# Scaling the residual on GpSimd in two passes, and two more early rounds of the search

## The reference

```python
x = x + _mixers(_rmsnorm(x, g_attn), w_in, g_out_a, g_out_b, sink_a, rpb_b, w_out)
h = _rmsnorm(x, g_ffn).reshape(B * S, D)      # (tokens, 1024)
return x + _expert_choice_ffn(h, w_router, w_gate, w_up, w_down).reshape(B, S, D)

def _expert_choice_ffn(h, w_router, w_gate, w_up, w_down):
    N, D = h.shape
    cap = CAP_FACTOR * N // N_EXPERTS         # 128 for the sample, 64 for the prompt
    aff = jax.nn.softmax(jnp.einsum('nd,de->ne', h, w_router).astype(jnp.float32), axis=-1)
    gate, idx = lax.top_k(aff.T, cap)
    xe = h[idx]
    ...
```

## Time and profile before

| | us |
|---|---|
| three runs | 2481.93, 2485.30, 2485.79 |
| median | 2485.3 |
| the profiled execution | 2484.71 |
| its span in the profile | 2482.9 |
| mixing, from its first own work to its last closing round | about 502 to 682 |
| the rest of the choice, up to the gather | about 682 to 696 |

### The profile page before, as it was taken

One profiled execution on the slowest core, in us unless ns is written; L12 is line 12 of the kernel. 1 busy time (PEld: TensorE's weight loads), 2 busy tenths in 40 slices (PEclk: granted clock), 3 DMA queues, 4 the chain that ended last, 5 costly groups with the idle time before them and its releaser, 6 DMA issues.

```text
span 2482.9 us, 43086 instructions
## 1 busy us (share of the span) xinstructions
PE 2434.5 (98%) x16395; PEld 2178.7 (88%) x16395; DVE 1673.5 (67%) x2432; ACT 1456.5 (59%) x2050; POOL 163.7 (7%) x172
## 2 busy tenths in 40 slices
PE   9999999999889999999999999999999999999997
PEld 7888877777579989899998989999998989999896
DVE  6355278854776767676666767666676767666677
ACT  4332189977555656556565656555565655656574
POOL 0000000000010101101010100101010110101010
PEclk9999999999989999999999999999999999999998
DMA  7353255354376767767676767767676776767696
GB/s 250 123 177 113 62 163 202 122 186 154 111 286 224 260 224 258 240 241 247 234 248 233 250 234 248 256 230 251 223 259 226 256 244 238 251 230 253 228 325 222
DMA packets 104549, 545.29 MB, mean 220 GB/s; under 512 B 11344, under 2 KB 19920, under 8 KB 54800
## 3 DMA queue, kind: packets, MB, share of 16 engines
q1 hardware_dynamic: 97072, 518.19, 59.6%
q0 software_dynamic: 7392, 25.96, 4.5%
HBM read 503.21 MB, written 40.89 MB: 219 GB/s over the span
## 4 chain that ended last, share of the span: by engine, by line
PE 69%; DVE 1%; DMA 1%; ACT 1%; issue 0%; POOL 0%; SPq 0%; DVEq 0%; ACTq 0%
PE ex_gate_ps L2043 16%; PE ex_up_ps L2043 16%; PE ex_gate_ps L2045 7%; PE ex_up_ps L2045 7%; PE ex_down_ps L2058 2%; PE ex_down_ps L2062 2%; PE ex_down_ps L2059 2%; PE ex_down_ps L2060 2%; PE ex_down_ps L2063 2%; PE ex_up_ps L2058 2%; PE ex_up_ps L2062 2%; PE ex_up_ps L2063 2%; PE ex_up_ps L2060 2%; PE ex_up_ps L2059 2%; DMA fi_x<-acc_scratch 1%; PE ex_turn_ps L2011 0%
## 5 line engine op out<-in xcount | busy, mean ns | idle before, releaser
L1879 DVE TENSOR_TENSOR ex_w_lo<-ex_w,ex_w_hi 128x2048 fp32r<-128x2048 f32 x384 | 879.8, 2292 | 440.5 <-ACT ex_w_hi L1775 437.1
L1775 ACT ACTIVATE ex_w_hi<-ex_w 128x2048 fp32r<-128x2048 f32 x384 | 733.4, 1910 | 208.7 <-PE ex_down_ps L2063 106.8
L2043 PE MATMUL ex_gate_ps<-ex_xt,ex_w_hi 128*128 128x384 f32 x2048 | 591.8, 359 | 0.7 <-DVE ex_xt L1885 0.7
L2043 PE MATMUL ex_up_ps<-ex_xt,ex_w_hi 128*128 128x384 f32 x2048 | 592.1, 359 | 0.0
L2045 PE MATMUL ex_up_ps<-ex_xt,ex_w_lo 128*128 128x192 f32 x2048 | 512.7, 250 | 0.0
L2045 PE MATMUL ex_gate_ps<-ex_xt,ex_w_lo 128*128 128x192 f32 x2048 | 512.7, 250 | 0.0
L2045 PEld LDWEIGHTS ex_gate_ps<-ex_xt,ex_w_lo 128*128 128x128 f32 x2048 | 391.1, 191 | 0.6
L2045 PEld LDWEIGHTS ex_up_ps<-ex_xt,ex_w_lo 128*128 128x128 f32 x2048 | 391.2, 191 | 0.0
L2043 PEld LDWEIGHTS ex_gate_ps<-ex_xt,ex_w_hi 128*128 128x128 f32 x2048 | 384.5, 188 | 1.6 <-issue 1.0
L2043 PEld LDWEIGHTS ex_up_ps<-ex_xt,ex_w_hi 128*128 128x128 f32 x2048 | 384.5, 188 | 0.0
L1797 ACT ACTIVATE ex_up_low<-ex_up_ps 128x384 f32<-128x384 f32 x128 | 62.9, 492 | 207.8 <-PE ex_up_ps L2045 207.8
(11 more groups left out here) (310 smaller groups left out, 4012.3 us busy)
## 6 DMA issues: line engine op xcount, KB each, us to landing
ex_w<-in_w_experts SPq DMA_DIRECT2D x384, 1024.0 KB, 4.8
pj_w<-in_w_in SPq DMA_DIRECT2D x54, 512.0 KB, 3.7
pj_xr<-in_xt SPq DMA_DIRECT2D x12, 512.0 KB, 6.0
o_scratch<-ld_out SPq DMA_DIRECT2D x24, 256.0 KB, 4.6
at_bias<-in_near_bias SPq DMA_DIRECT2D x4, 1536.0 KB, 8.8
q_p<-in_x SPq DMA_DIRECT2D x12, 512.0 KB, 4.5
acc_scratch<-k_p SPq DMA_DIRECT2D x12, 512.0 KB, 5.4
h_scratch<-q_p SPq DMA_DIRECT2D x12, 512.0 KB, 3.0
```

The lines of the kernel that those rows point to most:

```text
L1775: act.activation(w_hi[:, c % SLOTS, :], w[:, c % SLOTS, :], ACT.Copy).then_inc(hi_w, 1)
L1879: dve.tensor_tensor(w_lo[:, c % SLOTS, :], w[:, c % SLOTS, :], w_hi[:, c % SLOTS, :].bitcast(F32), ALU.subtract).then_inc(lo_w, 1)
L2043: nc.tensor.matmul(out[:, b, 0:2 * CAP], w_hi[:, slot, f], xt[:, k, :, :].rearrange("p h c -> p (h c)"), start=k == 0, stop=False)
```

## The change

`scale_h` is gone from VectorE. GpSimd makes `h` in two passes: once tile `t` is summed it multiplies by the gain, and once the root of tile `t` is refined it multiplies by `rs2` in place. VectorE waits for the second pass of the tile before, ahead of each root of tile `t`. Steps 10 and 11 do two rounds at the second place instead of one, so `EARLY` is 13. `gates` and `index` are allocated in the experts' stage and not for the whole kernel, which leaves room for the longer `best`.

```diff
-EARLY_ROUNDS = {S_TILES + 1: (1, 1, 1), S_TILES + 2: (1, 1, 1), S_TILES + 3: (1, 1, 1), S_TILES + 4: (1, 1, 0)}
+EARLY_ROUNDS = {S_TILES + 1: (1, 1, 1), S_TILES + 2: (1, 2, 1), S_TILES + 3: (1, 2, 1), S_TILES + 4: (1, 1, 0)}
...
-        summed = sem("mx_summed")
+        summed, gained = sem("mx_summed"), sem("mx_gained")
...
             pool.memset(route.lists[:], 0.0).then_inc(ready, 1)
+            for t in range(TILES):
+                if t >= 2:
+                    pool.wait_ge(h_out[t % 2], 16 * (t // 2))
+                if t == 0:
+                    pool.wait_ge(late_in, 64)
+                pool.wait_ge(summed, summed_with(t))
+                pool.tensor_tensor(h[t % 2], x2[t % 2], gain_ffn[:], ALU.mult).then_inc(gained, 1)
+                pool.wait_ge(gained, t + 1)
+                pool.wait_ge(refined, REFINE * (t + 2 + min(t + 1, TILES - 2)))
+                pool.tensor_scalar(h[t % 2], h[t % 2], rs2[:], None, ALU.mult).then_inc(normed2, 1)
...
-            def scale_h(t):
-                if t >= 2:
-                    dve.wait_ge(h_out[t % 2], 16 * (t // 2))
-                dve.scalar_tensor_tensor(out=h[t % 2], in0=x2[t % 2], scalar=rs2[:],
-                                         in1=gain_ffn[:], op0=ALU.mult, op1=ALU.mult).then_inc(normed2, 1)
-
...
                 if 0 <= t:
                     dve.wait_ge(root2, t + 1)
+                    if t:
+                        dve.wait_ge(normed2, t)
                     inverse_root(dve, refined, refines, ss2[:], rt2[:], [tmp2[:, i, :] for i in range(3)],
                                  rs2[:], 1.0 / D)
                     refines += REFINE
                     if t < LAST:
-                        scale_h(t)
                         search(s, 1)
...
-                    if t == LAST:
-                        scale_h(t)
                 search(s, 2)
```

## The result

The changed kernel takes 2490.9 us (median of eight runs, 2489.32 to 2492.91), the kernel before beside it 2483.85: 7.0 us more, a ratio of 1.0028 (95% interval 1.0017 to 1.0039). That is more than the 5 us that the prediction called the least one can tell, and the median lies in its range of 2484 to 2496. The profiled execution took 2492.07 us and its span is 2490.3 us, against 2482.9 before. The helper `inverse_root` now stands at L212 to L221, the addition at L1274, `merged` at L1201, the softmax at L1318 to L1327, its turning at L1423. GpSimd's product is L1120, its second pass L1123.

The account below looks back on a forecast made before the run. TensorE was taken to set the pace in steps 1 to 10, VectorE's search after the last projection. 2.2 + 1.9 + 2.7 + 1.7 - 0.3 - 1.6 + 0.2 = +6.8 us, median 2492, range 2484 to 2496.

Parts of the forecast that it names:

- GpSimd's product and its stop: In the mixing, GpSimd's 2.41 us product holds VectorE's inverse root until it ends; 0.24 per step, +1.9 in steps 2 to 9.
- Step 1: First mixing step: the stopped root delays TensorE's transposes of `merged`, +2.2; a second low clock stretch, +1.7, only as upper bound.
- The second pass, 1.2 us: GpSimd's multiplication of `h` by a column of scalars, taken as 1.2 us with the memset as nearest row.
- That is covered.: `h` reaches its store 1.5 to 2 us later; SP's queued load of `o` has its reader a step later, no cost.
- The 1.8 that the prediction booked for the stopped root in step 10: Step 10: the first root, stopped by GpSimd's product, ready at 646.71 instead of 644.92, part of the step's +2.7.
- The fall of the clock in step 10, +1.7: Step 10: behind TensorE's pauses of 1.0 and 1.7 us the clock falls as in step 1, +1.7.
- Step 12: Last step: stopped affinities +0.2, VectorE's dropped pass -0.3; behind it, two wide rounds become narrow, -1.6.
- (a): Rival, not slower: the root's tiny instructions slip past GpSimd's product; -1.0 us, 2484.3; chance 0.12.
- (c): Rival: the search on VectorE is stopped too, +5 more, 2497, or GpSimd pays for each change of operation; chance 0.08.
- (d): Rival: the experts' gather, 1.6 us sooner, queues behind the last weights; sum 8.4; chance within the forecast's 0.60.
- (b): Rival, partly: same stops in the mixing but a shorter product or no fall of the clock; +1 to +5 us; chance 0.20.
- The lower bound: Case of a 1.29 us product: 1.1 in step 1, nothing in 2 to 9, 1.8 in 10, no clock fall; +1.2.

Follow-up runs that it names:

- ports: Probe without the layer: ten small VectorE instructions started one by one under GpSimd's product, scaling pass and memset (2.34, 2.85 and 1.80 us); no kernel time.
- pool_only: The changed kernel with the early rounds as before (11 instead of 13): 2491.46 us, ratio 1.0033 to the kernel before.
- o_first: The changed kernel, but SP issues the load of `o` for tile t + 3 ahead of its wait for `h`: 2491.49 us, ratio 1.0030.
- late_o_first: The changed kernel with the diffs of `late_product` and `o_first` joined: 2483.94 us, ratio 1.0000 to the kernel before.
- late_product: The changed kernel with GpSimd's product moved behind the step's second root for tiles 0 to 9: 2503.44 us, ratio 1.0074.
- rounds_only: The kernel before, VectorE still scaling, with only the two added early rounds and the moved `gates` and `index`: 2488.22 us, ratio 1.0018.

## Why the prediction came out as it did

Direction and size were right (+7.0 against +6.8), but that the size is so close is partly luck: errors in both directions cancel, and in step 10 the wait that was booked is not the wait that came.

- **GpSimd's product and its stop.** Right. The product took 2.40 us for the 2.41 worked out, started 0.15 behind the addition (0.13), and stopped the two-column operation until its end. Steps 2 to 9 each paid 0.27, for 0.24; eight of them are 2.2 us. By the Trainium skill (SBUF — State Buffer, Who interferes with whom) the second engine is blocked for the other's whole instruction: the product agrees, the scaling pass doesn't (1.12 of 2.85 us in `ports`), so there the measurement decides.
- **Step 1.** The mechanism was right and the size too small. The stall was 2.0 for 2.2, since the product began 0.16 behind the addition (519.18 + 1.40 to 520.74) and not behind L1293 (L1288 before), which ended 0.18 later. But the clock was then low for 6.8 us and not 3.4. The prediction kept that as a bound, +1.7; it cost 0.9, so the step was worth 2.9. `pool_only`, the same program up to there, had the short stretch: the 0.9 belongs to the profiled execution and not surely to every run.
- **The second pass, 1.2 us.** Wrong: 2.85, outside the bounds of 0.96 and 2.58 that the memset and the product gave. Of the rows to choose from, the memset was the least alike.
- **"That is covered."** This is the step that failed. The store of `h` came 2.4 us later in most steps (8.73 instead of some 6.3 behind the addition), for the 1.5 to 2 of the prediction. SP's queue has the load of `o` behind the store of `h`, and with the stopped root and a second pass of 2.85 in step 9 the load left 3.62 us ahead of the next addition, and took 4.3. In step 10 ScalarE stood for 2.0 us. The 1.8 that the prediction booked for the stopped root in step 10 didn't happen; this took its place, and `o_first` shows that either gives nearly the same step (16.47 and 16.64). The 0.9 of the added round was right (+1.0 in `late_o_first`).
- **The fall of the clock in step 10, +1.7.** Wrong: at pauses of the weight loads of 1.30 us (for `merged`) and 2.00 (at L1423) the clock stayed at 1.00. The prediction took the fall over from step 1, where the weight loads had paused for 1.75. That step doesn't carry over: in `late_product` the same pause of 1.75 in step 1 brought no fall either, while pauses of 1.82 to 1.88 later did. The fall did come in step 10 of `rounds_only`, behind 2.60 us.
- **Step 12.** The +0.2 for the stopped last affinities was 0: at 685.34 L1327 came 1.0 us behind the start of the pass (684.33) and kept its 0.23, as `ports` would have it. The -0.3 and the -1.6 were right to a tenth.
- **The rivals.** (a) is out: the operations on two columns don't slip past the product (1.17 for 0.15 in step 9). (c) is out, the search isn't stopped, and a change of operation on GpSimd costs nothing to be seen: in `late_product` the product ends at 587.21 + 2.39 = 589.60 and the next pass starts at 589.71. (d) is out: the way from the picked places to the first matmul grew by 0.1 only. (b) named the missing fall of the clock, one of its two conditions, but not what made up for it.
- **The lower bound.** The case of a product of 1.29 us keeps the 1.8 of step 10, though a product shorter by 1.12 ends sooner there too: 0.7 and the 0.9 of the round make 1.6, and the sum is +1.0 and not +1.2. Nothing hangs on it.

The terms that fell away are 1.7 and 0.2 us. Those not foreseen are 0.7 in step 1 (0.9 for the clock, 0.2 less for the stall), 0.3 in steps 2 to 9, 0.3 in step 10, 0.8 ahead of the first addition and 0.5 behind the rounds. The last two are no larger than the differences between profiles of these kernels in stretches that they share; without them the forecast was 0.7 us too high for the part that the change touches.

## What to carry to other kernels

Moving work to an idle engine frees only the time that the sender's order can use. Here VectorE had slack, and what was moved stopped the six tiny instructions that TensorE waits for; look at what the sender does in the moment at which the other engine will start, not at its load. A result that becomes later delays all that is queued behind its store: write down the next load in that queue, its lead over its reader and its time to land, before calling it covered. Price the pauses with the clock that may fall behind them, and don't take that fall as certain. And where two delays end at the same wait, removing one shows nothing; take away both before giving the idea up.

## What the runs showed of the hardware

- GpSimd's TENSOR_SCALAR with a column of scalars takes 2.85 us for 128x1024, more than the product of two tensors (2.40), and stops VectorE only in its first 1.12 us, the stopped instruction's own 0.15 among them. Why it lets go then, these runs don't show.
- A GpSimd product of 2.34 us turned a VectorE operation on two columns from 0.15 into 1.90 us; on one column TENSOR_SCALAR isn't stopped. A memset on GpSimd stops TENSOR_SCALAR on two and more columns (1.33) but not an operation with two SBUF inputs (0.16).
- TensorE's clock fell to the lower level behind pauses of its weight loads of 1.75 (step 1 of the kernel before), 1.82, 1.84, 1.88, 2.07 and 3.33 (`late_product`), 2.60 (`rounds_only`) and 3.74 us, and stayed at the upper one behind pauses of 1.30 and 2.00 in step 10 of the changed kernel and of 1.75 in step 1 of `late_product`. The length of the pause alone doesn't tell. The time at half clock was about 3.4 us behind most of them, and 6.8 behind the 3.33 and the 3.74; but in `pool_only` it was 3.4 behind 3.74 too, so the same pause can cost either.
